# Decoder layer on one core: the compression's first products as runs of 256 and 288 columns, one head group to a PSUM slot

## What is computed

```python
def compress(k_raw, w1, b1, w2):
    B, T, G, Dh = k_raw.shape
    nb = (T - CMP_BLOCK) // CMP_STRIDE + 1
    n_str = nb + CMP_RATIO - 1
    s = k_raw[:, :n_str * CMP_STRIDE].reshape(B, n_str, CMP_STRIDE, G, Dh)
    w1r = w1.reshape(CMP_RATIO, CMP_STRIDE, Dh, Dh)
    pre = jnp.einsum('bnlgd,lde->bnge', s[:, 0:nb], w1r[0]) + b1
    for r in range(1, CMP_RATIO):
        pre = pre + jnp.einsum('bnlgd,lde->bnge', s[:, r:r + nb], w1r[r])
    return jnp.einsum('bnge,ef->bngf', jax.nn.silu(pre), w2)
```

## Time and profile before

| What | us |
|---|---|
| Median of three runs | 840.41 |
| The three runs | 836.99, 840.41, 842.74 |
| Span of the profiled execution (first to last instruction) | 835.7 |

### The profile page before, as it was taken

One profiled execution on the slowest core, in us unless ns is written; L12 is line 12 of the kernel. 1 busy time (PEld: TensorE's weight loads), 2 busy tenths in 40 slices (PEclk: granted clock), 3 DMA queues, 4 the chain that ended last, 5 costly groups with the idle time before them and its releaser, 6 DMA issues.

```text
span 835.7 us, 11541 instructions
## 1 busy us (share of the span) xinstructions
PE 778.5 (93%) x4479; PEld 534.8 (64%) x4479; DVE 375.9 (45%) x799; ACT 221.1 (26%) x480; POOL 168.2 (20%) x270
## 2 busy tenths in 40 slices
PE   5999999997999989999999999999999899998773
PEld 3657778674756657777777777774456755555431
DVE  2201999899778881102006552231237522231106
ACT  2001324152256662233025640000001112221113
POOL 2348447010110006000004520002000212232100
PEclk9999999999999999999999999999999999999979
DMA  9775446130180005152214539703106999999737
GB/s 302 174 17 182 143 101 166 25 122 1 50 292 2 2 2 178 51 176 76 75 51 127 179 89 294 285 1 113 50 26 235 380 374 411 407 403 391 304 137 259
DMA packets 87505, 138.98 MB, mean 166 GB/s; under 512 B 25493, under 2 KB 60465, under 8 KB 86287
## 3 DMA queue, kind: packets, MB, share of 16 engines
q1 hardware_dynamic: 71439, 101.41, 35.5%
q0 software_dynamic: 11392, 32.71, 13.2%
q10 hardware_dynamic: 4616, 4.08, 1.6%
HBM read 132.00 MB, written 21.14 MB: 183 GB/s over the span
## 4 chain that ended last, share of the span: by engine, by line
PE 79%; DMA 9%; DVE 6%; issue 3%; SPq 1%; ACTq 0%; ACT 0%; DVEq 0%; POOLq 0%; POOL 0%
PE ps L1915 18%; PE ps L2105 15%; PE ps L2363 7%; PE ps L2441 6%; PE ps L1939 5%; PE ps L2012 4%; PE ps L2457 3%; DMA mgT<-w_up 2%; PE ps L2148 2%; PE ps L2123 2%; DMA arena<-w_up 2%; PE ps L2136 2%; DMA mgT<-w_in 2%; DMA arena<-yscratch 2%; PE ps L2431 1%
## 5 line engine op out<-in xcount | busy, mean ns | idle before, releaser
L2105 PE MATMUL ps<-xT,keep 128*128 128x288 f32 x512 | 126.9, 407 | 0.8 <-ACT h L1206 0.5
L2105 PEld LDWEIGHTS ps<-xT,keep 128*128 128x128 f32 x512 | 96.5, 190 | 27.4 <-ACT h L1206 0.9
L1915 PE MATMUL ps<-xT,arena 128*128 128x288 f32 x384 | 95.4, 407 | 0.0
L1915 PEld LDWEIGHTS ps<-xT,arena 128*128 128x128 f32 x384 | 72.1, 190 | 19.2
L1395 DVE SCALAR_TENSOR_TENSOR cv<-keep,cv 128x512 f32<-128x512 f32 x120 | 83.7, 748 | 1.4
L2363 PE MATMUL ps<-arena,xT 128*128 128x512 f32 x128 | 55.4, 592 | 0.0
L2441 PE MATMUL ps<-keep,mgT 128*64 128x256 f32 x224 | 41.8, 390 | 4.9 <-DMA mgT<-w_up 3.2
L1939 PE MATMUL ps<-mgT,xT 128*128 128x512 f32 (+1 forms) x128 | 43.5, 498 | 1.2 <-DMA mgT<-w_in 1.2
L2363 PEld LDWEIGHTS ps<-arena,xT 128*128 128x128 f32 x128 | 24.2, 190 | 29.3 <-issue 29.2
L836 ACT ACTIVATE mgT<-ps 64x512 f32<-64x512 f32 x56 | 33.2, 593 | 32.2 <-PE ps L1993 31.6
L1276 ACT ACTIVATE keep<-h 128x1024 f32<-128x1024 f32 (+1 forms) x5 | 5.3, 1059 | 130.1 <-DVE h L1706 121.5
(11 more groups left out here) (412 smaller groups left out, 1340.1 us busy)
## 6 DMA issues: line engine op xcount, KB each, us to landing
arena<-w_down SPq DMA_DIRECT2D x19, 512.0 KB, 16.8
keep<-w_in SPq DMA_DIRECT2D x16, 512.0 KB, 3.8
arena<-w_gate SPq DMA_DIRECT2D x15, 512.0 KB, 8.5
arena<-w_up SPq DMA_DIRECT2D x15, 512.0 KB, 12.5
keep<-w_gate SPq DMA_DIRECT2D x14, 512.0 KB, 10.4
keep<-w_up SPq DMA_DIRECT2D x14, 512.0 KB, 17.6
h<-x_prompt SPq DMA_DIRECT2D x8, 512.0 KB, 5.4
arena<-w_in SPq DMA_DIRECT2D x8, 512.0 KB, 7.5
```

The costliest lines, as they stand in the source:

```text
L1915: last = mm(tokens(j)[:, b, :], weights(k), halves(x[:, k, :])[:, b, :], start=k == 0, stop=k == n_k - 1)
L2105: last = mm(out[:, 0:half], wmg[n // 2 % 3][:, k, :], xT[:, k, (n % 2) * half:(n % 2 + 1) * half], start=k == 0, stop=k == KD - 1, skip_gr ...
```

## The change

The jobs, their slots and their order stay. `w1` now holds all 544 strides of head group 0 and `w1own` those of head group 1. A group's strides stand in columns 256 to 799 of its slot, so that 256 of them lie in the first bank and 288 in the second, and they are one piece for a reader. TensorE fills them as 8 products of 256 columns and 8 of 288. ScalarE copies the upper half of a group in one instruction of 64x544. VectorE does the samples' and the prompt's sums group by group and gives a slot back after each group. The waits on `s_upper` count as before, two to a compression.

```diff
+        def first_job(n, g):
+            return JOB[("w1", "w1own")[g], n]
+
+        def strides_at(j):
+            return slot(j)[:, 512 - STR_S // 2:512 - STR_S // 2 + STR]
...
             def upper_halves(n):
-                j = JOB["w1", n]
-                take(act, j)
-                nc.scalar.activation(upper[:, :, 0:STR_S], slot(j)[HD:P, :].rearrange("p (g n) -> p g n", g=NKV), ACT.Copy).then_inc(s_upper, 1)
-                j = JOB["w1own", n]
-                take(act, j)
-                nc.scalar.activation(upper[:, :, STR_S:STR], slot(j)[HD:P, 0:2 * STR_P].rearrange("p (g n) -> p g n", g=NKV), ACT.Copy).then_inc(s_upper, 1)
+                for g in range(NKV):
+                    j = first_job(n, g)
+                    take(act, j)
+                    nc.scalar.activation(upper[:, g, :], strides_at(j)[HD:P, :], ACT.Copy).then_inc(s_upper, 1)
...
             def compress_pre(n):
-                j = JOB["w1", n]
                 dve.wait_ge(s_pads, 3)
-                take(dve, j)
-                dve.wait_ge(s_upper, 2 * n + 1)
+                by_block = lambda x: x[:, 0:STR_S].rearrange("p (b n) -> p b n", b=DB)
                 for g in range(NKV):
...
+                    j = first_job(n, g)
+                    take(dve, j)
+                    dve.wait_ge(s_upper, 2 * n + g + 1)
+                    lo = strides_at(j)[0:HD, :]
+                    V.scalar_tensor_tensor(by_block(pre[:, g, :])[:, :, 0:NCS], by_block(lo)[:, :, 0:NCS], b1[:, n:n + 1],
+                                           by_block(upper[:, g, :])[:, :, 1:NCS + 1], ALU.add, ALU.add)
+                    give(V.scalar_tensor_tensor(pre[:, g, STR_S:STR_S + NCP], lo[:, STR_S:STR_S + NCP], b1[:, n:n + 1],
+                                                upper[:, g, STR_S + 1:STR_S + 1 + NCP], ALU.add, ALU.add), j)
...
             def compress_first(n):
-                j = JOB["w1", n]
                 pe.wait_ge(s_w1, 32 * (n + 1))
                 result_of(pe, *[JOB["raw", n, u] for u in range(4, DB)], JOB["own", n])
-                claim(pe, j)
                 for g in range(NKV):
-                    for k in range(KD):
-                        last = mm(slot(j)[:, g * 512:(g + 1) * 512], w1[:, k, :], XT[:, g, k, 0:STR_S], start=k == 0, stop=k == KD - 1)
-                fill(last, j)
-                j = JOB["w1own", n]
-                claim(pe, j)
-                for g in range(NKV):
-                    for k in range(KD):
-                        last = mm(slot(j)[:, g * STR_P:(g + 1) * STR_P], w1[:, k, :], XT[:, g, k, STR_S:STR], start=k == 0, stop=k == KD - 1)
-                fill(last, j)
+                    j = first_job(n, g)
+                    claim(pe, j)
+                    for lo, hi in ((0, STR_S // 2), (STR_S // 2, STR)):
+                        for k in range(KD):
+                            last = mm(strides_at(j)[:, lo:hi], w1[:, k, :], XT[:, g, k, lo:hi], start=k == 0, stop=k == KD - 1)
+                    fill(last, j)
```

More of the change, by code:

```diff
@@ L1429, in compress_pre @@
             def compress_pre(n):
-                j = JOB["w1", n]
                 dve.wait_ge(s_pads, 3)
-                take(dve, j)
-                dve.wait_ge(s_upper, 2 * n + 1)
+                by_block = lambda x: x[:, 0:STR_S].rearrange("p (b n) -> p b n", b=DB)
                 for g in range(NKV):
[L1435 to L1438, removed]
-                j = JOB["w1own", n]
-                take(dve, j)
-                dve.wait_ge(s_upper, 2 * n + 2)
-                for g in range(NKV):
-                    last = V.scalar_tensor_tensor(pre[:, g, STR_S:STR_S + NCP], slot(j)[0:HD, g * STR_P:g * STR_P + NCP], b1[:, n:n + 1],
-                                                  upper[:, g, STR_S + 1:STR_S + 1 + NCP], ALU.add, ALU.add)
-                give(last, j)
+                    j = first_job(n, g)
[6 more added lines that the diff above has]
+                                                upper[:, g, STR_S + 1:STR_S + 1 + NCP], ALU.add, ALU.add), j)
             def rotated(c):
```

## The result

| | us |
|---|---|
| Changed kernel, median of 7 runs | 831.75 (829.77 to 833.98) |
| Kernel before beside it, median of 7 runs, the three above among them | 837.96 (835.47 to 842.74) |
| Ratio | 0.993, 95% interval 0.9908 to 0.9951 |
| Spans of the profiled executions, after and before | 828.0 and 835.7 |

The interval goes from 4.1 to 7.7 us, so the forecast difference is at its edge. The two profiled spans differ by 7.7 us. The question is what the rest is.

What follows compares the result with a forecast made beforehand. TensorE bounds the first compression, VectorE the way to the second, then TensorE again; gains of 1.6 us (first call) and 2.55 us (second) make 4.15 us, so 840.41 becomes 836.3 us, range 832.3 to 841.5.

Steps and rivals of the forecast that it cites:

- The 256-column step: TensorE's compression products: 256 columns step 0.216 us, at most 0.2425; a call falls from 17.22 to 14.67 us.
- The rival with loads that aren't hidden: In compress_first, 256 columns don't cover weight loads: TensorE gains nothing, +0.95 us, 841.4 us; chance 0.05.
- I charge the loads nothing: Compression products: weight loads of 0.19 us are hidden by the record before and add no time.
- The way through VectorE: First compression: of TensorE's 2.55 us only 1.6 arrive, since VectorE carries the chain up to the second call.
- Tail 0.95 us longer: First call, behind the last product: ScalarE's copy goes from 0.22 to 0.62 us, VectorE's sums from 0.32 to 0.86.
- Second call: Second compression: starts 1.6 us earlier, at 195.4, and takes 16.4 instead of 18.97 us, all 2.55 us passed on.
- Wait at the third query projection: TensorE, after the first compression, waits 0.7 us for a slot that VectorE frees.
- Behind it nothing: After the compressions, attention, routing and experts cost nothing extra; the 4.15 us pass through to the end.
- The rival of a swallowed gain: Experts' stage: if transfers' start alone sets its weight stream, up to all 4.15 us go, 840.4 us; chance 0.08.
- I assume the same stretch once more: Second compression: 3.4 us at half clock after TensorE's idle time, costing 1.7 us, as before.
- The spell over the whole call: Rival: half clock for the whole second compression costs 13 us more, 849 us; chance 0.02.
- it becomes 840.41 - 4.15 = 836.3 us: Whole kernel: forecast time, from the 840.41 us median of three runs less the 4.15 us gain.

Runs made afterwards that it cites:

- e_s128: Changed kernel with each group's 544 strides split into runs of 128 and 416 columns instead of 256 and 288; ratio to the kernel before 0.9946.
- e_s32: Changed kernel with each group's 544 strides split into runs of 32 and 512 columns instead of 256 and 288; ratio to the kernel before 1.0043.
- e_bwarm: Kernel before, without the change, plus 30 transposes of the identity in TensorE's idle time ahead of the second compression; ratio to the kernel before 0.9998.
- e_bwarm2: Kernel before with the 30 transposes ahead of the second compression, measured once more; ratio to the kernel before 0.9993.
- e_warm: Changed kernel plus 30 transposes of the identity into a free slot in TensorE's idle time ahead of the second compression; ratio to the kernel before 0.9902.
- e_s64: Changed kernel with each group's 544 strides split into runs of 64 and 480 columns instead of 256 and 288; ratio to the kernel before 1.0001.
- e_only0: Kernel before with the change made in the first compression only; ratio to the kernel before 0.9968.

## Why the prediction was wrong, and what of it was right

The mechanism in the compression and its size held. The time did not, and it failed by 0.55 us at the edge of the range.

- *The 256-column step.* 0.216 us by the line, 14.67 us for a call: measured 14.67. The other splits show the line from both sides. The rival with loads that aren't hidden is refuted: e_s128 has 128-column records with a load each, and takes 14.75 us. The Trainium skill's rule ("TensorE: Matmul & The Clock Gate", packing small matmuls, what overlaps and what doesn't) that a load overlaps only when row groups differ doesn't hold for these products. "I charge the loads nothing" is right for records of 128 columns and more. For the short ones it hides what they pay for: by the steps of L2385 above, the 0.109 us go with the load.
- *The way through VectorE.* Tail 0.95 us longer: 0.97 in e_s32, where it stands alone. Second call 1.6 us earlier: 1.67. Wait at the third query projection 0.7: 0.62. Slack at the values' evacuation 0.4: 0.40.
- *Second call.* 2.55 us one to one; at full clock the whole stage is 4.24 us shorter, forecast 4.15.
- *Behind it nothing.* The middle from 269.8 us on is the same to 0.02 us in all profiles, and the end scatters around the same length. The rival of a swallowed gain is refuted.
- *The clock.* "I assume the same stretch once more" was off: 6.8 us of half clock, 2.3 us lost instead of 1.7, in the first profile, 3.4 to 6.8 in the others. The spell over the whole call didn't come. The sum had no second stretch at the attention's start; the first profile of the kernel before has one that costs 1.5 us, all four of the changed kernel one of 1.0 to 1.5 us, so it hardly moved this comparison.
- *The step that failed* is "it becomes 840.41 - 4.15 = 836.3 us". The level was taken from the median of three runs of the kernel before. In five later series of 17 to 29 runs each its median was 836.4 to 837.2 us, so the base was 3 to 4 us too high. From 836.7 the sum gives 836.7 - 4.15 = 832.55 us, and the changed kernel's medians were 831.75 to 833.85. The prediction read the distance of the runs from the profiled span, 1.3 to 7.0 us, as what lies around the span. In every later run with both numbers on record an execution's time is 1.7 to 2.0 us above its own span, so the profiled execution of 835.7 us took about 837.5 us, and the sum on it gives 833.3 us. The rest of the 4.7 us was scatter between executions: the profiled spans of the 18 runs made later lie at most 3.7 us below their medians, more than half of them less than 1.9. The range allowed 2.5 us for this scatter, less than the error of the base.
- The first ratio, 0.993, is larger than the forecast by 1.7 us. The first changed profile shows where such luck comes from: an end of 190.3 us that the later ones (194.0, 193.7, 196.1) do not repeat.

Two things stay open. The transposes gain 3.2 us in the changed kernel and 0.2 and 0.6 us, by the ratios, in the kernel before. The trace of e_bwarm fits this, 168.77 us to the attention's last turning against 168.82 and 169.07, since the clock fell elsewhere. That of e_bwarm2 does not: it has 165.61 us, 3.2 us less, where the time gained 0.6. It has 10.2 us of half clock at the routing, between 639 and 671 us, which neither profile of the kernel before has, but e_warm has as much there and is faster. Why the gain does not reach the time in this kernel is not shown. And which executions get slow product groups in the experts' stage was not tried.

## What to carry to other kernels

A float32 product with a weight load of 128 columns of its own costs the same from 32 to 128 columns here, so split a long run so that no piece is below 128 columns; an uneven split pays a whole load's step for each short piece. With a load of 64 columns the floor was lower, 0.059 us. When a result is cut into parts, the last part's readers become the tail: count their copy and sums, and give the reader other work between the parts. For a change of half a per cent take the level from many runs, or from the profiled execution's own time, and not from a median of three that lies far above it; compare stages record by record and at equal clock, and widen the range by the scatter of the base.

## What the runs showed of the hardware that was not expected

- The floor under short float32 records goes with the columns of the weight load: 36-column records step 0.106 us with a load of 128 columns and 0.059 us with one of 64 (L2385 in the kernel before).
- The half clock at the second call is not of fixed length: 3.4 or 6.8 us in the eleven profiles without transposes whose call began with 128 or more columns a record, 10.2 us in both that began with 32 or 64 columns (e_s32, e_s64, one profile each).
- The clock can fall in the midst of an unbroken stream, as at 213.2 us in e_only0 and at 162.5 and 213.7 us in e_bwarm, among or right behind 32-column records, but also at 226.8 us in the first profile of the changed kernel, 2.4 us into an unbroken run of the attention's products.
- After 30 transposes the call of e_warm ran at a granted clock of 1.00 from its start. So did the second call's start in all seven profiles with the transposes; in all thirteen without them a half-clock stretch lay over it.
- The experts' stage of one kernel differs by up to 6 us between executions, with product groups of 32 records at 3.7, 5.4 or, in the kernel before, 6.5 us.
